# A two-block model on one core: split pool and index tiles, four banks in turn, key halves by a permutation, and chunk keys scaled ahead of exponents

## The reference

```
# first block
proj = rmsnorm(x) @ w_in            # 512 pool | 256 query latent | 128 key latent | 32 key rope
x1, x2 = k_rope_raw[..., :16], k_rope_raw[..., 16:]
k_rope = concat(x1*cos - x2*sin, x2*cos + x1*sin)
# second block
proj = h @ w_in_2                   # ... | ckv 128 | ... | iq 8x64 | ik 64 | iw 8
rel   = einsum('bqhd,bsd->bqhs', iq, ik)
score = einsum('bqh,bqhs->bqs', iw, relu(rel))      # then the best 128 keys of each query
qkv   = silu(causal_conv(qkv)); q = l2norm(q); k = l2norm(k)
decay = exp(where(causal, gc_i - gc_j, -inf))
lmat  = where(strict, (kb @ k.T) * decay, 0)        # inverted chunk by chunk
kg    = k * exp(gc_last - gc)
```

## Time and profile before

| | us |
|---|---|
| median of 3 runs | 1989.54 (1987.36 to 1990.73) |
| profiled execution | 1985.49 |
| its span | 1983.7 |
| PE busy | 1868.6 (94%) |
| DVE busy | 1504.7 (76%) |
| ACT busy | 1132.4 (57%) |
| POOL busy | 192.7 (10%) |

### The profile page before, as it was taken

One profiled execution on the slowest core, in us unless ns is written; L12 is line 12 of the kernel. 1 busy time (PEld: TensorE's weight loads), 2 busy tenths in 40 slices (PEclk: granted clock), 3 DMA queues, 4 the chain that ended last, 5 costly groups with the idle time before them and its releaser, 6 DMA issues. The chain is left out here.

```text
span 1983.7 us, 24552 instructions
## 1 busy us (share of the span) xinstructions
PE 1868.6 (94%) x8419; PEld 1400.0 (71%) x8420; DVE 1504.7 (76%) x1684; ACT 1132.4 (57%) x1208; POOL 192.7 (10%) x199
## 2 busy tenths in 40 slices
PE   6978978999999999999999999999998999988998
PEld 3346456787778877777777777777774467867983
DVE  4146666999899998999999899899897266795532
ACT  4233315777677777777777777677665344334510
POOL 0031210000000000000000000000044001003410
PEclk9988978999999999999999999999998979997999
DMA  7100836999999999999999999999987202201001
GB/s 212 61 24 14 332 145 224 365 372 358 373 368 357 376 369 359 376 366 367 379 355 376 378 356 371 368 353 369 375 311 252 92 28 79 85 1 65 1 22 43
DMA packets 102005, 499.72 MB, mean 252 GB/s; under 512 B 18609, under 2 KB 35230, under 8 KB 51682
## 3 DMA queue, kind: packets, MB, share of 16 engines
q1 hardware_dynamic: 94898, 473.37, 62.6%
q0 software_dynamic: 7056, 25.69, 3.7%
HBM read 478.57 MB, written 20.46 MB: 252 GB/s over the span
## 5 line engine op out<-in xcount | busy, mean ns | idle before, releaser
L1627 DVE TENSOR_TENSOR part<-ring,part 128x2048 fp32r<-128x2048 f32 x380 | 857.9, 2290 | 111.4 <-ACT part L1348 109.7
L1348 ACT ACTIVATE part<-ring 128x2048 fp32r<-128x2048 f32 x380 | 729.1, 1921 | 334.5 <-DMA ring<-in_w_gate_up 199.7
L1477 PE MATMUL bank<-part,xT_hi 128*128 128x512 f32 x2048 | 536.9, 404 | 18.1 <-DVE xT_lo L1658 13.3
L1477 PEld LDWEIGHTS bank<-part,xT_hi 128*128 128x128 f32 x2048 | 382.7, 190 | 113.1 <-issue 26.7
L1488 PE MATMUL bank<-part,actT_hi 128*128 128x512 f32 x1024 | 280.4, 396 | 1.6 <-DVE rest L1637 0.7
L1477 PE MATMUL bank<-part,xT_lo 128*128 128x512 f32 x1024 | 281.9, 397 | 0.0
L1477 PEld LDWEIGHTS bank<-part,xT_lo 128*128 128x128 f32 x1024 | 195.0, 190 | 46.3
L1488 PEld LDWEIGHTS bank<-part,actT_hi 128*128 128x128 f32 x1024 | 190.1, 188 | 43.8 <-DVE part L1627 1.2
L1488 PE MATMUL bank<-part,actT_lo 128*128 128x512 f32 x512 | 159.4, 393 | 0.0
L1771 POOL DMA_INDIRECT rest<-h_rows,rest x33 | 41.8, 1266 | 1115.2 <-PE bank L1460 1030.6
L1488 PEld LDWEIGHTS bank<-part,actT_lo 128*128 128x128 f32 x512 | 96.3, 188 | 21.5
(11 more groups left out here) (463 smaller groups left out, 2315.8 us busy)
## 6 DMA issues: line engine op xcount, KB each, us to landing
ring<-in_w_gate_up SPq DMA_DIRECT2D x256, 1024.0 KB, 7.2
ring<-in_w_down SPq DMA_DIRECT2D x128, 1024.0 KB, 6.9
expert_rows<-rest SPq DMA_DIRECT2D x31, 512.0 KB, 7.6
ring<-in_w_in SPq DMA_DIRECT2D x14, 1024.0 KB, 5.2
rest<-in_w_ada SPq DMA_DIRECT2D x8, 1536.0 KB, 6.7
ring<-in_w_out SPq DMA_DIRECT2D x16, 512.0 KB, 5.1
ring<-in_w_in SPq DMA_DIRECT2D x8, 464.0 KB, 6.9
rest<-in_x SPq DMA_DIRECT2D x4, 512.0 KB, 5.9
```

The source lines that it names most:

```text
L1348: nc.scalar.activation(hi[part(i, c)], raw(c), ACT.Copy).then_inc(sig("hi_ready"), counts)
L1477: ins = nc.tensor.matmul(bank[g][:], rows[:, c, :], w[:, g * 512:(g + 1) * 512], start=first, stop=last, skip_group_check=True)
L1627: V.tensor_tensor(lo[part(i, c)], raw(c), hi[part(i, c)].bitcast(F32), ALU.subtract).then_inc(sig("lo_ready"), counts)
```

## The change

- First block: the turns use banks 0 to 3. `w_in` is loaded in two sets of columns, latents ahead of pool. The second rope tile is gone: ACT copies the 32 rope rows out, and TensorE multiplies them with a 32x32 permutation (`swap`, from the identity, by POOL) after the first pool tile. The four pool tiles are split like those of the second block: ACT makes `hT_hi` and `u_hi`, VectorE `hT_lo` and `u_lo`, ahead of the latent variance. The raw bias rows are loaded behind `w_out`.
- Second block, head: tile 0 is plain as before, the index key tile comes second, then bias rows and small products, then the other three index query tiles, split. The small chains of the decay move ahead of the scores on ACT and VectorE, and so do the turns of `ckv`. The third and fourth half of the columns are loaded after the bias rows.
- Scores: four banks (2, 3, 5, 0); TensorE waits for the relu four back, before two back.
- Convolution tiles: `qk_sum` of tile n after tile n + 2, before after tile n + 1.
- Chunks: `scale_k(t)` ahead of the exponents of chunk t + 2.

```diff
-                ins = nc.tensor.transpose(bank[k % 2][:, t * P:(t + 1) * P], xn[:, t, k * P:(k + 1) * P], ident)
+                ins = nc.tensor.transpose(bank[k % 4][:, t * P:(t + 1) * P], xn[:, t, k * P:(k + 1) * P], ident)
...
             for k in range(KT):
-                sp.dma_start(w_in[:, k, :], a["w_in"][0, k * P:(k + 1) * P, :]).then_inc(sig("w_in_loaded"), 16)
+                sp.dma_start(w_in[:, k, D_POOL:], a["w_in"][0, k * P:(k + 1) * P, D_POOL:]).then_inc(sig("w_in_loaded"), 16)
+            for k in range(KT):
+                sp.dma_start(w_in[:, k, 0:D_POOL], a["w_in"][0, k * P:(k + 1) * P, 0:D_POOL]).then_inc(sig("w_in_pool_loaded"), 16)
...
-            project(bank[5][64:96, :], krope_w, 0, ROPE)
...
-                project(bank[2 + g % 2][:], w_in, g * P, P)
+                if g == 0:
+                    pe.wait_ge(sig("A_hT_lo"), 2)
+                    pe.wait_ge(sig("A_w_lo"), 2)
+                o = slice(g * P, (g + 1) * P)
+                for k in range(KT):
+                    for w, h in ((u_hi, hT_hi), (u_lo, hT_hi), (u_hi, hT_lo)):
+                        ins = nc.tensor.matmul(bank[2 + g % 2][:], w[:, k, o], h[k // 4][:, k % 4, :], start=(k == 0 and h is hT_hi and w is u_hi), stop=(k == KT - 1 and h is hT_lo))
+                ins.then_inc(sig("proj_done"), 1)
+                if g == 0:
+                    pe.wait_ge(sig("swap_ready"), 1)
+                    pe.wait_ge(sig("k_rope_copied"), 1)
+                    nc.tensor.matmul(bank[5][64:96, :], swap[64:96, :], k_rope[64:96, :], start=True, stop=True).then_inc(sig("k_swapped"), 1)
...
+            for n in range(2):
+                nc.scalar.activation(hT_hi[n], hT[:, 4 * n:4 * n + 4, :], ACT.Copy).then_inc(sig("A_hT_hi"), 1)
+            act.wait_ge(sig("w_in_pool_loaded"), 16 * KT)
+            for n in range(2):
+                nc.scalar.activation(u_hi[:, 4 * n:4 * n + 4, :], w_in[:, 4 * n:4 * n + 4, 0:D_POOL], ACT.Copy).then_inc(sig("A_w_hi"), 1)
             act.wait_ge(sig("angles_ready"), 1)
...
-            dve.wait_ge(sig("proj_done"), 5)
+            dve.wait_ge(sig("k_swapped"), 1)
...
+    INDEX_BANKS = (2, 3, 5, 0)
...
-            for n in range(2):
-                pe.wait_ge(sig(f"slot_loaded{n}"), 16)
-                for c in range(2):
-                    tile(2 * n + c, halves[n], c * P, P)
+            pe.wait_ge(sig("slot_loaded0"), 16)
+            tile(0, halves[0], 0, P)
+            pe.wait_ge(sig("w_small_loaded"), 48)
+            tile(1, w_small, 0, DI)
...
+            split_tile(0, 1)
+            split_tile(1, 0)
+            pe.wait_ge(sig("ckv_ready"), 1)
+            for q in range(T):
+                ins = M.transpose(bank[4][:, q * P:(q + 1) * P], ckv[:, q, :], ident)
+            ins.then_inc(sig("ckv_turned"), 1)
+            split_tile(1, 1)
...
-                if i >= 2:
-                    pe.wait_ge(sig("relu_ready"), i - 1)
+                if i >= 4:
+                    pe.wait_ge(sig("relu_ready"), i - 3)
...
             for n in range(12):
+                if n == 1:
+                    pe.wait_ge(sig("relu_ready"), 3 * HI)
                 split_tile(2 + n // 2, n % 2)
-                if 1 <= n <= 8:
-                    qk_sum(n - 1)
+                if 2 <= n <= 9:
+                    qk_sum(n - 2)
...
             for t in range(T):
+                scale_k(t)
                 if t + 2 < T:
                     exp_diff(t + 2)
                     exp_rows(t + 2)
-                scale_k(t)
```

More of the change, by code:

```diff
@@ L490, in _ @@
                 if n == 2:
+                    act.wait_ge(sig("proj_done"), 4)
+                    nc.scalar.activation(k_rope[64:96, :], bank[4][64:96, :], ACT.Copy).then_inc(sig("k_rope_copied"), 1)
                     act.wait_ge(sig("lat_summed"), 1)
@@ L2318, in _ @@
             A.sem_inc(sig("ckv_squares"), 1)
[L2320 to L2329 removed]
+            copy_iq(1)
+            make_hi(2)
             act.wait_ge(sig("ab_ready"), 1)
@@ L2335, in _ @@
             A.activation(s2, s2, ACT.Exp, scale=-1.0).then_inc(sig("ab_exp"), 1)
+            copy_iq(2)
+            act.wait_ge(sig("ckv_turned"), 1)
+            A.activation(ckvT, bank[4][:], ACT.Copy).then_inc(sig("ckvT_ready"), 1)
+            copy_iq(3)
+            for i in range(3 * HI):
+                t = 1 + i // HI
+                n = (t + 1) * P
+                if i == 8:
+                    make_hi(3)
+                act.wait_ge(sig("index_done"), i + 1)
+                if i >= 2:
+                    act.wait_ge(sig("relu_read"), i - 1)
+                A.activation(relu[:, i % 2, 0:n], bank[INDEX_BANKS[i % 4]][:, 0:n], ACT.Relu).then_inc(sig("relu_ready"), 1)
             act.wait_ge(sig("taps_zero"), 1)
@@ L2540, in _ @@
                 r = slice(64 * (h % 2), 64 * (h % 2) + 64)
[L2541 to L2548 removed]
+                if i >= 4:
+                    pe.wait_ge(sig("relu_ready"), i - 3)
+                M.matmul(bank[INDEX_BANKS[i % 4]][:, 0:(t + 1) * P], iqT[r, h // 2, t * P:(t + 1) * P], ikT[r, 0:(t + 1) * P], start=True, stop=True).then_inc(sig("index_done"), 1)
             pe.wait_ge(sig("small_ready"), 1)
@@ L2913, in _ @@
             V.tensor_scalar(g, g, -1.0, None, ALU.mult).then_inc(sig("g_ready"), 1)
+            make_lo(2)
+            for i in range(3 * HI):
+                t, h = 1 + i // HI, i % HI
+                n = (t + 1) * P
+                dve.wait_ge(sig("relu_ready"), i + 1)
+                if h == 0:
+                    V.tensor_scalar(score[t], relu[:, i % 2, 0:n], w_index[:, t, 0:1], None, ALU.mult).then_inc(sig("relu_read"), 1)
+                else:
+                    dve.wait_ge(sig("relu_read"), i)
+                    V.scalar_tensor_tensor(out=score[t], in0=relu[:, i % 2, 0:n], scalar=w_index[:, t, h:h + 1], in1=score[t], op0=ALU.mult, op1=ALU.add).then_inc(sig("relu_read"), 1)
+                if h == HI - 1:
+                    dve.wait_ge(sig("relu_read"), i + 1)
+                    chain.link(V.tensor_tensor(score[t][:, t * P:n], score[t][:, t * P:n], negmask, ALU.add))
+            make_lo(3)
             GONE = -3.0e38
```

147 lines of the change are left out of this document (66 added, 81 removed).

## The result

| | kernel before | changed kernel |
|---|---|---|
| median of the runs, us | 1988.95 (4 runs, 1987.36 to 1990.73) | 1941.67 (4 runs, 1939.88 to 1944.37) |
| profiled execution, its time and span, us | 1985.49, 1983.7 | 1944.37, 1942.5 |
| mean granted clock | 0.962 | 0.972 |

The change makes the kernel 47.3 us faster: ratio 0.9766, 95% interval 0.9741 to 0.9791. A second set of five runs beside other kernels gave 0.9765 (0.9739 to 0.9792). Forecast were 1946 us and a range of 1936 to 1965.

The account below looks back on a forecast made before the run. TensorE was taken as the engine others wait for, except at three places where it is held back. Gains of 11 + 11.1 + 12 + 9.5 = 43.6 us gave a median of 1946 us, from 1989.54; range 1936 to 1965.

Parts of the forecast that it names:

- Block 1: First block through the pool tiles: permutation for the second rope projection, split pool tiles, fewer transpose waits; 11 us gained.
- Head: Second block up to the scores: split index query tiles gain 3.8 us, partly given back; scores start 1.0 us earlier.
- Scores: Index scores on four banks take 17.2 us, before 26.2; the first convolution tile behind takes 6.4, before 7.4.
- Convolution and gate tiles: Second block's convolution tiles: with the sum two tiles behind, a pair takes 13.65 us, before 16.37; 12 us gained.
- TensorE reaches the gate tiles 12 us earlier: End of the convolution tiles: TensorE, two tiles ahead and no longer limiting, arrives at the gate tiles 12 us earlier.
- the 10 us of slack lets it catch up the last 2.6: Gate tiles: VectorE, busy 61.97 of 72 us, uses its 10 us of slack to catch up 2.6.
- Chunks: Chunk stage: keys scaled ahead of the exponents end two 4 us waits; 10.7 us, 9.5 taken for low clocks.
- 2: Rival, chunk stage: the new order gives nothing, since VectorE's difference is met next anyway; 1955.5 us, 8%.
- 5: Rival, block 1: remainders delay the variance, stalling latent sum and pool tiles by 5 us; 1951 us, 6%.
- 1: Rival, expert stage: a weight stream setting its own end swallows block 1's gain; 1957 us, 10%.
- 3: Rival, convolution tiles: the clock swings, each low start costing 1.6 us, 12 in all; 1958 us, 12%.
- 4: Rival, slower: TensorE stays at 1.2 GHz from the scores through all twelve convolution tiles; 2002 us, 2%.

Follow-up runs that it names:

- e9: Changed kernel with ACT's rounding of the next weight half behind the last score, not between scores 7 and 8; median 1937.41 us, ratio 0.9746.
- e2: Changed kernel with two banks in turn for the index scores, TensorE waiting for the relu two back; median 1956.49 us, ratio 0.9833.
- e3: Changed kernel with the sum of squares of a convolution tile one tile behind it again, not two; median 1954.19 us, ratio 0.9829.
- e1: Changed kernel with ACT again scaling chunk t's keys behind the exponents of chunk t+2; median 1951.04 us, ratio 0.9815.
- e6: Changed kernel with block 1's four pool tiles plain fp32 again, without their rounded parts and remainders; median 1948.03 us, ratio 0.981.
- e12: e10 with block 1 as in the kernel before; median 1945.26 us, ratio 0.9799.
- e8: Changed kernel with four relu buffers, separate banks for the bias rows and an early start of the scores; median 1936.67 us, ratio 0.9735.
- e10: Changed kernel with the edits of both e8 and e9; median 1937.02 us, ratio 0.9739.
- e11: Kernel before with the changed block 1 alone, block 2 as before; median 1974.73 us, ratio 0.9922.
- e7: Changed kernel with block 1's transposes on two banks in turn again; 1938.93 us, ratio 0.975.

## Why the prediction was right

**Block 1 (11; measured 10.8 at the pool tiles).** The sum was right with terms off both ways: permutation 4.9 for 5.5 with its loss, split tiles 5.6 for 5.1, the rest about 0.4 for 0.6. That the variance, root and first pool copy just keep ahead of the third tile held: TensorE waits in none of the pool tiles.

**Head (1.0; 1.3).** The 1.0 us of wait for the bias rows was 0.89, that for the last copy 0.69. Over the changed kernels the head lay between 43.8 and 45.1.

**Scores (17.2 and 6.4; 16.2 and 5.9).** The term was too small by 1.6 us, 1.0 of it because I laid a third of the way to the low clock, where VectorE was the pace and the clock cost nothing. That the stretch came to the 16.2 of the full clock is in part luck: the clock did fall, and without the pause it is 15.0 (e9). e2 shows what I had only half priced: the banks also decide whether the clock comes back. The 3.4 us at the low clock that remained came behind a pause that my sum had named (ACT's rounding, 1.2 us lost by VectorE, measured 1.25) but not tied to the clock; e9 ties it. The Trainium skill (TensorE: Matmul & The Clock Gate, "A second HAM failure mode: psum-queue depth-cycling") has the clock swing where TensorE idles for short spells between groups of matmuls that cycle through banks. This trace agrees that the clock falls behind such a spell; that this speaks against four banks was my reading, and it was wrong: two banks stayed at 0.50 (e2), and four came back.

**Convolution and gate tiles (12; 10.8).** The pair of copies (13.56 for 13.65), TensorE's own pair (12.95 for 13.1) and VectorE's end (75.9 for 77) were right. The step that failed is "TensorE reaches the gate tiles 12 us earlier", for which the prediction has no sum, and with it "the 10 us of slack lets it catch up the last 2.6". Counted from the first copy TensorE reaches them 10.8 us earlier, and from there to the chunks it is 81.0 us in both kernels, whatever VectorE's slack: TensorE is the full engine there (70.90 of 72 us busy). Counted from the start of the first convolution tile the gain is 12.4 us (86.6 and 74.2), but 1.7 of that is this tile itself, which the scores' term already has; whether the 12 came from there isn't shown. The window over the stage gives the size at once: 8.0 us of idle time and 3.2 by the clock, 11.2 us (an estimate; by the matmuls' busy times it is 12.4, of which 1.7 remain).

The Trainium skill's figure (same page, "Back-to-back issue gap") of 216 ns is, by that section, the gap of an isolated matmul; for a stream with a weight load for each matmul it gives about 131 ns. This trace has neither: 233 ns a pass, with as many weight loads as passes (x696 for x698 in the window of e3).

**Chunks (9.5; 10.2).** By hand it was 10.7, 20.2 us to the next stage; 20.7 came. The discount for low clocks wasn't needed: none came up to the next stage.

**Rivals.** 2 and 5 are out by e1 and e6. Of 1 a part may hold (e12). 3 didn't come: the clock is 1.00 over the convolution tiles, and it is the order before that had 0.98. 4 didn't come.

**Sum.** 10.8 + 13.0 + 10.8 + 10.2 + 0.6 = 45.4 us against 43.6 forecast, 41.2 between the two profiled executions and 47.3 by the medians. In part the terms offset each other (scores 1.6 too small, convolution tiles 1.2 too large), and that the median came within 5 us of the forecast is luck, since the stretch between the blocks alone moves by more.

## What to carry to other kernels

For a stage where one engine is nearly full, take its idle time and its time at the low clock from one window over the stage: that is about what a reordering can give, and here it gave nearly all of it. Follow that engine through the stage, not the pace of its neighbours: the copies stood 13.56 us a pair apart while TensorE went on at 12.95 and set the end. When a stage of 1137 us scatters by 13, judge a change of 10 us by the length of its own stage between two instructions; the scores, the convolution tiles and the chunks here repeat to 0.1 us. A job that holds up the producer is covered by more buffers (e8, 2.9 us) or moved out of the way (e9, 1.2 us); with the buffers in place moving it gave 0.1 us more (e10).

## What the runs showed of the hardware

In the scores the granted clock fell to its lower level behind a pause of TensorE of 1.27 us. With four banks it came back after 3.4 us (the changed kernel, and every profile with four banks and the pause, eight in all), with two it stayed at 0.50 for 20 to 24 us, into the first convolution tile (e2, and the kernel before and e11, where the pause is one of 1.5 us), and it didn't fall where the pause was taken out (e9, e10, e12).

The clock between two parts also differs from one execution to the next of the same block 1. In the changed kernel's first profile and in e3's, with pool tiles ending at 79.1 and 78.8 us, the stretch ahead of the attention was

```profile
90.00:100.00 10.00, 6.05 (x11) 2.46 (x10) 0.00 (x0) 7.19 (x13) 0.00 (x0) 0.75 0.49 130
100.00:110.00 10.00, 8.40 (x17) 3.06 (x15) 4.17 (x7) 0.60 (x1) 0.00 (x0) 0.91 0.00 0
```

```profile
90.00:100.00 10.00, 6.06 (x15) 2.45 (x14) 0.00 (x0) 7.43 (x14) 0.00 (x0) 1.00 0.46 119
100.00:110.00 10.00, 5.51 (x13) 1.93 (x11) 6.96 (x11) 0.00 (x0) 0.00 (x0) 1.00 0.00 0
```

and the attention began at 114.2 in the one and 111.3 in the other, 35.1 and 32.6 us behind the pool tiles: 2.6 us, of which TensorE's rows show 1.8 in one group of four matmuls (3.78 for 1.99 us) and 0.8 in the next (2.67 for 1.88). The fourteen profiles agree: 32.6 us where the clock stayed high up to the attention (e3), 34.1 to 34.3 with 3.4 us at the low clock (ten), 35.1 to 35.4 with 6.8 (the changed kernel, e8 and e12).

The experts' stage, without an edit near it, took 1135.0 us in e7 and 1146.0 in e8:

```profile
286.00:1421.00 1135.00, 1116.56 (x5114) 890.75 (x5115) 1023.06 (x823) 812.73 (x637) 39.18 (x31) 0.99 0.93 362
```

```profile
287.00:1433.00 1146.00, 1119.36 (x5112) 892.67 (x5113) 1023.13 (x824) 812.72 (x636) 40.94 (x31) 0.99 0.93 358
```

The rate (362 and 358 GB/s) is only the same bytes over the longer time. That the bytes came late shows in ACT's waits for the expert weights, of e7 and of e8 (us in total, times, longest):

```profile
ACT part L1387 <- DMA ring<-in_w_gate_up: 186.6, 191, 4.4
ACT part L1387 <- DMA ring<-in_w_down: 102.2, 90, 4.2
```

```profile
ACT part L1387 <- DMA ring<-in_w_gate_up: 195.8, 189, 4.6
ACT part L1387 <- DMA ring<-in_w_down: 107.6, 93, 3.5
```

They are 14.6 us more in e8, and a weight DMA took 6.7 us from issue to landing for 6.5 (median). Why it took longer in one execution the runs don't show.
